# Retention group norm moved into the tile loop of a two-layer RetNet and HGRN2 decoder step

## The reference, cut to what matters

```python
mu = jnp.mean(o, axis=-1, keepdims=True)
var = jnp.mean(jnp.square(o - mu), axis=-1, keepdims=True)
on = (o - mu) * lax.rsqrt(var + GN_EPS) * gn_g.reshape(RET_HEADS, RET_DV)
o = jax.nn.silu(g) * on.reshape(bsz, l, RET_V)
return o @ w_out, s
```

## Time and profile before

| | |
|---|---|
| median of 3 runs | 1620.12 us (1617.95 to 1620.16) |
| profiled execution | 1618.11 us, span 1616.3 us |
| TensorE | busy 1570.4 us, 97% of the span |
| VectorE | 621.4 us, 38% |
| ScalarE | 422.5 us, 26% |
| mean granted TensorE clock | 0.998 of full speed |
| moved by DMA | 514.93 MB, 319 GB/s over the span |

### The profile page before, as it was taken

How to read it: one execution, slowest core, us unless ns; L and a number is a source line. 1 busy time by engine, 2 the same in 40 slices (tenths; PEclk the granted TensorE clock), 3 DMA queues, 4 the chain that set the end, 5 groups by cost and what they waited for, 6 DMA issues and landing times.

```text
span 1616.3 us, 32138 instructions
## 1 busy us (share of the span) xinstructions
PE 1570.4 (97%) x14356; PEld 931.8 (58%) x14356; DVE 621.4 (38%) x942; ACT 422.5 (26%) x608; POOL 79.7 (5%) x107
## 2 busy tenths in 40 slices
PE   7999999999999988999999999999999999999997
PEld 7888887999999988973333333333333333333332
DVE  6566576576655899542121101101111011011114
ACT  4444554444445475741000000010000000100001
POOL 1122221000000012001000000000000000000001
PEclk9999999999999999999999999999999999999999
DMA  9577879445455455269999999999999999999993
GB/s 357 211 274 294 293 269 395 169 157 182 152 179 193 157 170 178 101 269 344 428 413 405 429 402 398 426 415 409 424 394 429 421 392 425 420 396 426 390 428 131
DMA packets 138232, 514.93 MB, mean 319 GB/s; under 512 B 6700, under 2 KB 61172, under 8 KB 129780
## 3 DMA queue, kind: packets, MB, share of 16 engines
q1 hardware_dynamic: 117780, 447.93, 70.4%
q0 software_dynamic: 15824, 57.97, 9.7%
q10 hardware_dynamic: 4496, 7.02, 1.2%
HBM read 472.43 MB, written 40.47 MB: 317 GB/s over the span
## 4 chain that ended last, share of the span: by engine, by line
PE 85%; DVE 8%; ACT 1%; issue 1%; DMA 1%; POOL 0%; ACTq 0%; DVEq 0%
PE ps L1905 83%; DVE ring_low_parts L1338 1%; DVE ring L1387 1%; PE ps L2051 1%; DVE ring L1641 1%; DMA ring<-in_state_retention 1%; ACT ring_low_parts L980 1%; DVE arena L1631 1%; DVE ring L1614 0%; DVE ring L1613 0%; DVE ring L1586 0%; DVE arena L1333 0%; DVE arena L1565 0%; ACT ring L1103 0%; DVE expert_arena L1872 0%
## 5 line engine op out<-in xcount | busy, mean ns | idle before, releaser
L1905 PE MATMUL ps<-ring,expert_x_turned 128*32 128x448 f32 x5376 | 508.1, 539 | 0.0
L1905 PEld LDWEIGHTS ps<-ring,expert_x_turned 128*32 128x32 f32 x5376 | 174.5, 110 | 330.7 <-issue 330.7
L1905 PE MATMUL ps<-normed_high,ring_low_parts 128*128 128x264 f32 x1344 | 265.9, 289 | 6.7 <-DVE arena L1333 3.0
L1905 PE MATMUL ps<-ring,expert_hidden_turned 128*32 128x512 f32 x2496 | 269.3, 592 | 0.0
L980 ACT CAST ring_low_parts<-ring 128x1024 fp32r<-128x1024 f32 (+2 forms) x180 | 180.0, 1001 | 241.9 <-PE ps L1905 240.8
L1338 DVE TENSOR_TENSOR ring_low_parts<-ring,ring_low_parts 128x1024 fp32r<-128x1024 f32 (+2 forms) x180 | 207.9, 1163 | 76.4 <-ACT ring_low_parts L980 76.4
L1905 PEld LDWEIGHTS ps<-normed_high,ring_low_parts 128*128 128x128 f32 x1344 | 216.0, 190 | 8.2 <-issue 3.6
L1837 DVE TENSOR_TENSOR expert_arena<-expert_arena,ps 128x1344 f32<-128x1344 f32 x16 | 24.9, 1554 | 504.5 <-PE ps L1905 504.5
L1905 PEld LDWEIGHTS ps<-ring,expert_hidden_turned 128*32 128x32 f32 x2496 | 81.1, 110 | 185.8 <-issue 185.8
L1905 PE MATMUL ps<-normed_low,ring_low_parts 128*128 128x264 f32 x640 | 160.5, 286 | 0.0
L1905 PE MATMUL ps<-h_parts,ring_low_parts 128*128 128x264 f32 x1056 | 130.0, 285 | 0.2 <-DVE h_parts L1322 0.2
(11 more groups left out here) (290 smaller groups left out, 1185.2 us busy)
## 6 DMA issues: line engine op xcount, KB each, us to landing
ring<-in_moe_w_gate SPq DMA_DIRECT2D x64, 1792.0 KB, 13.4
ring<-in_moe_w_down SPq DMA_DIRECT2D x48, 2048.0 KB, 16.9
ring<-in_moe_w_up SPq DMA_DIRECT2D x48, 1792.0 KB, 14.2
expert_piece_slot<-in_moe_w_up SPq DMA_DIRECT2D x16, 1792.0 KB, 15.1
ring<-in_ret_w_in SPq DMA_DIRECT2D x8, 2048.0 KB, 11.0
ring<-in_state_retention POOLq DMA_DIRECT2D x32, 512.0 KB, 7.1
out_ret_s<-ring POOLq DMA_DIRECT2D x32, 512.0 KB, 4.2
ring<-in_hg_w_in SPq DMA_DIRECT2D x8, 2048.0 KB, 7.9
```

What stands on the lines that cost most here:

```text
L1905: return nc.tensor.matmul(out, lhsT, rhs, start=first, stop=last)
```

## The change

- For heads 0 to 2 the group norm moves into the loop. `NORM_TILE` says after which tile each of its four TensorE steps comes: head 0 after 18, 19, 21, 22, head 1 after 27, 29, 30, 33, head 2 after 37, 38, 39, 40.
- A sum over a head is now made in two steps: `mup` (and `vap` for the squares) multiplies the head's four tiles by 32 columns each, every tile into its own column group of one bank; ScalarE copies the bank to `std`; then `mu` (`var`) multiplies by ones over all 128 rows, which adds up the four parts and gives every row the sum. So the four spreading matmuls and `rowsel` go. In layer 1, `hsel` takes the place of `rowsel`.
- Root and reciprocal run for each head (`norm_root` on ScalarE, `normalized` on VectorE, in `group_std`). `group_std` lies where GpSimd will put its zeros, so GpSimd waits for the scaling of the last head (`scaled_ok`).
- The gate of heads 0 to 2 is one operation a tile (gate times gain times `oT`) in place of gain times gate and a multiplication over the head. High and low parts of heads 0, 1 and 2 are made in tiles 37 and 38, 41 and 42, 45 and 46.
- The last head's norm comes behind the loop, interleaved with the output projection. Its blocks are reordered: tiles 0 to 3 with k 0 to 5 and k 6 to 11 (heads 0 to 2), then (0, k 12 to 15), (1, 12 to 15), (2, 12 to 15), (4, 0 to 7), (3, 12 to 15), (4, 8 to 15), then tiles 5 to 7 in halves.
- The three `keep_busy` of the group norm go; that ahead of the dense layer stays.

```diff
+for _h, _tiles in enumerate(((18, 19, 21, 22), (27, 29, 30, 33), (37, 38, 39, 40))):
+    for _kind, _t in zip(("mup", "mu", "vap", "var"), _tiles):
+        NORM_TILE[(_kind, _h)] = _t
+NORM_BANK = {("mup", 0): 4, ("mu", 2): 4, ("var", 2): 4, ("mup", 3): 4, ("vap", 3): 4, ("mu", 3): 6, ("var", 3): 6}
...
-        for i in range(8):
-            for k in (0, 8):
-                blocks.append((("wo", i), ("rwo", i // 2), 0, 256, 16, P * (i % 2), k, k + 8, 0))
+        for i, k0, k1 in [(i, k0, k0 + 6) for i in range(4) for k0 in (0, 6)] + \
+                [(0, 12, 16), (1, 12, 16), (2, 12, 16), (4, 0, 8), (3, 12, 16), (4, 8, 16)] + \
+                [(i, k0, k0 + 8) for i in range(5, 8) for k0 in (0, 8)]:
+            blocks.append((("wo", i), ("rwo", i // 2), 0, 256, 16, P * (i % 2), k0, k1, 0))
...
             filled(pool, ("sot", RH - 1))
+            pool.wait_ge(scaled_ok, RH)
             nc.gpsimd.memset(hq_pad, 0.0).then_inc(hq_zero, 1)
...
+            def norm_part(kind, h):
+                filled(act, (kind, h))
+                frees(A.copy(std[:, :], bank((kind, h))[:, 0:NT]), (kind, h))
+            def norm_square(h):
+                freed(act, ("mu", h))
+                A.activation(o_sq, oT[:, 4 * h:4 * h + 4, :], ACT.Square).then_inc(sq_ok, 1)
+            def norm_root(h):
+                filled(act, ("var", h))
+                if h:
+                    act.wait_ge(scaled_ok, h)
+                frees(A.activation(group_std, bank(("var", h))[:, 0:NT], ACT.Sqrt, bias=eps_g), ("var", h))
...
+            norm_part("mup", last)
+            for n in range(W0, F0):
+                if n == W0 + 2:
+                    norm_part("vap", last)
+                    norm_root(last)
+                if n == W0 + 4:
+                    act.wait_ge(scaled_ok, RH)
+                    head_high(last)
+                high_part(n + FPL)
+                if n == W0:
+                    norm_square(last)
+                    A.activation(table_mark[:, 0:1], eps_n, ACT.Sqrt)
...
+                if j < 4 * RH - 4:
+                    i = V.scalar_tensor_tensor(out=oT[:, j, :], in0=oT[:, j, :], scalar=gain, in1=gT[:, j, :],
+                                               op0=ALU.mult, op1=ALU.mult)
+                else:
+                    i = V.tensor_scalar(gT[:, j, :], gT[:, j, :], gain, None, ALU.mult)
...
+            def centred(h):
+                filled(dve, ("mu", h))
+                frees(V.tensor_tensor(o_head(h), o_head(h), bank(("mu", h))[:, 0:NT].unsqueeze(1).to_broadcast([P, 4, NT]),
+                                      ALU.subtract), ("mu", h))
+            def normalized(h):
+                freed(dve, ("var", h))
+                link(V.reciprocal(group_std, group_std))
+                V.tensor_tensor(o_head(h), o_head(h), group_std.unsqueeze(1).to_broadcast([P, 4, NT]), ALU.mult)\
+                    .then_inc(scaled_ok, 1)
...
+                if kind in ("mup", "vap"):
+                    claim(name)
+                    for e in range(4):
+                        x = oT[:, 4 * h + e, :] if kind == "mup" else o_sq[:, e, :]
+                        i = mm(ps[32 * e:32 * e + 32, FILL[name][0], 0:NT], col_gn[:, 0, :], x)
+                else:
+                    freed(pe, ("mup" if kind == "mu" else "vap", h))
+                    claim(name)
+                    i = mm(bank(name)[:, 0:NT], ones, std[:, :])
+                close(i, name)
...
+            norm_product("mup", RH - 1)
+            for n in range(W0, F0):
+                ready = (lambda k: pe.wait_ge(o_ok, k // 4 + 1)) if n in (W0, W0 + 1, W0 + 8) else None
+                between = (lambda: norm_product("mu", RH - 1)) if n == W0 else \
+                    (lambda: norm_product("vap", RH - 1)) if n == W0 + 2 else None
+                product(n, o_hi, o_lo, ready, between)
+                if n == W0 + 2:
+                    norm_product("var", RH - 1)
```

More of the change, by code:

```diff
@@ L221, in retention_fills @@
             add((("sot", g), 5))
+        for name in norms_after(t, "mup", "mu", "vap", "var"):
+            add((name, NORM_BANK.get(name, 5)))
     for t in range(8 * RH + 16):
         retention_fills(t)
[L225 to L229, removed]
+    for kind in ("mup", "mu", "vap", "var"):
+        add(((kind, RH - 1), NORM_BANK[(kind, RH - 1)]))
     for i in range(8):
@@ L1049, in _ @@
                         A.activation(S, S, ACT.Copy, scale=GAMMA[hd]).then_inc(unit_decayed, 1)
[L1050 to L1072, removed]
+                for kind, hd in norms_after(t, "mup", "vap", "var"):
+                    if kind == "var":
+                        norm_root(hd)
+                    else:
+                        norm_part(kind, hd)
+                if h == RH and j in (5, 9, 13):
+                    act.wait_ge(gated_ok, j // 4)
+                    head_high(j // 4 - 1)
+            last = RH - 1
+            norm_part("mup", last)
[10 more added lines that the diff above has]
+                    A.activation(table_mark[:, 0:1], eps_n, ACT.Sqrt)
+                if block_closes(n):
+                    i = blocks[n][0][1]
+                    freed(act, ("wo", i))
+                    gain_high(1, h_hi, i)
+                    if i % 2:
+                        square(1, i // 2)
             for n in range(F0, F1):
@@ L1474, in _ @@
                           ("sot", hd))
[L1476 to L1500, removed]
@@ L1501, in _ @@
-            for i in range(9):
-                if i < 8:
+                for _, hd in norms_after(t, "mu"):
+                    centred(hd)
+            gate(4 * RH - 1)
+            last = RH - 1
+            centred(last)
+            pending = []
+            for n in range(W0, F0):
+                i = blocks[n][0][1]
+                if n == W0 + 1:
+                    dve.wait_ge(gated_ok, RH)
+                    dve.wait_ge(sq_ok, RH)
+                    link(V.tensor_tensor(o_head(last), o_head(last), gT[:, 4 * last:4 * last + 4, :], ALU.mult))
+                if n == W0 + 2:
+                    normalized(last)
+                if n == W0 + 4:
+                    head_low(last)
+                if block_closes(n):
@@ L1934, in mean_square, with product @@
                 close(i, ("ms", n))
-            def product(n, x_hi, x_lo, ready=None):
+            def product(n, x_hi, x_lo, ready=None, between=None):
                 name, _, _, _, _, _, k0, k1, base = blocks[n]
@@ L2089, in _ @@
                     sample_turn(hd)
[L2090 to L2116, removed]
+                for kind, hd in norms_after(t, "mup", "mu", "vap", "var"):
+                    norm_product(kind, hd)
+            norm_product("mup", RH - 1)
+            for n in range(W0, F0):
+                ready = (lambda k: pe.wait_ge(o_ok, k // 4 + 1)) if n in (W0, W0 + 1, W0 + 8) else None
+                between = (lambda: norm_product("mu", RH - 1)) if n == W0 else \
+                    (lambda: norm_product("vap", RH - 1)) if n == W0 + 2 else None
+                product(n, o_hi, o_lo, ready, between)
+                if n == W0 + 2:
+                    norm_product("var", RH - 1)
             for n in range(F0, F1):
```

75 lines of the change are left out of this document (55 added, 20 removed).

## The result

The changed kernel takes 1636.55 us in the median of four runs (1632.0 to 1645.71). The kernel before, run beside it, takes 1619.29. The ratio is 1.0103, with a 95% interval of 1.0078 to 1.0128. That is slower, and 14.2 us above the forecast of 1622.3; it lies outside the range of 1607 to 1627.

The account below looks back on a forecast made before the run. TensorE was taken as the bound in retention, with VectorE as full around the group norm. Terms 64.8 - 70.9 + 8.6 - 0.3 = +2.2 us took the median from 1620.12 to 1622.3; range with rival 1: 1607 to 1627.

Parts of the forecast that it names:

- the big term: Before output tile 6: the fourth weight piece, beside the zeros at 0.0925 MB/us, comes late and TensorE idles 12.1 us.
- 2.75 us of issue and landing: Fourth output piece: time added to its 22.7 us transfer, derived from a piece loaded alone in 8.2 us.
- Clock: Behind the idle time before output tile 6, a half-speed stretch costs 2.0 us, with bounds 1.7 and 3.4.
- the old slow stretch: Output projection of the kernel before: 3.4 us at half speed, costing 1.7 us, counted as removed.
- The tiles: Retention tiles: added norm matmuls and waits, less absorbed waits, cost 8.6 us by the last gate tile; bounds 5 and 14.
- fetch of a sample state: Retention loop near 215: its two waits and lost matmul overlap, 3.3 us together, taken as gone.
- A packed group: Group norm sums: four matmuls of 264 columns on four column groups, taken as 0.6 us.
- The later stages: Dense layer's first block: one cast's subtraction less before the last low part, -0.3 us.
- rival 2: Tiles 37 to 47: VectorE doesn't keep up, pair 15 waits for memory, 5 us more, 1628; chance 0.09.
- rival 3: Packing fails for these shapes: 8 groups at 1.2 us more, 1632; chance 0.02.
- The table loads: ScalarE: four added loads hidden behind TensorE work, except a quarter microsecond in tile 34.
- The norm's removal: Between retention and output projection: 21.2 us of group norm, a 1.04 us wait and slow clock go, 23.9 us.

Follow-up runs that it names:

- experiment 1: Changed kernel with the buffer of zeros moved to other memory, so GpSimd's store does not wait for the last head; 1628.7 us, ratio 1.0044.
- experiment 2: Changed kernel with GpSimd's zeros held until the last output tile is done; 1630.1 us, ratio 1.0049.
- experiment 3: Kernel before, with only GpSimd's zeros held back until output tile 0 is done; 1635.32 us, ratio 1.0078.
- experiment 5: Changed kernel with the zeros stored in five parts of 2 MB, each issued when a weight piece has landed; 1619.28 us, ratio 0.9972.
- experiment 4: Changed kernel with the zeros asked for in rows of 256 values, meant to give 1 KB packets; 1639.4 us, ratio 1.0114.
- Experiment 6: On experiment 5: head 0's mean in another bank, heads 0 and 1 scaled after the pair update, low parts later; 1610.98 us, ratio 0.9915.

## Why the prediction failed

**The mechanism of the big term was right, its size was not.** The forecast had TensorE idle before tile 6, ended by a cast that waits for the fourth piece, with zeros beside it packet for packet; experiments 1, 2, 3 and 5 show the store as the cause. The step said that the piece is there 25.4 us after its request and that TensorE then idles 12.1 us. Measured: 32.74 and 19.35, 7.2 us more. Of the piece's extra 7.3 us, the transfer made 3.3: summed by microseconds its last packet left near 311, so 2.1 MB took 26.0 us, 0.081 MB/us, where I had 0.0925 and 22.7 us. My packet of the other queue had 3.7 KB, from retention states; a packet of zeros has 4.1. The rest, 4.0 us, is in the term that I took as 2.75 us of issue and landing. It was 4.4 us until the first packet and 2.4 from the last packet to the landing: I had taken it from a load that met no full queue. With the store out of the way (experiment 5) the median fell by 24.9 us, from 1644.19 to 1619.28; the wait and its clock are 21.5 of it, and the other 3.4 are not assigned.

**Clock.** I let the clock fall once, behind the long wait, for 2.0 us; 2.2 were measured. But I also had waits of 1.8 and 1.85 us in my own sum, and the earlier trace rows show such a wait with a fall behind it. In the profiled execution the waits of 2.14 and 2.06 us brought a fall each, 1.7 us twice. This step was missing. I subtracted the old slow stretch and did not ask what its successors would bring. A fall is not certain, though: six profiles have these four waits in the tiles (the changed kernel twice, experiments 1, 2, 4 and 5), and the clock fell behind 6 of the 12 waits of 2.1 us and behind 1 of the 12 of 1.7. In experiment 1, for one, TensorE waited 2.08 us until 254.68, and the mean granted clock from 255 to 259 was 1.00. So by these counts a wait of 2.1 us brought 0.9 us of slow clock on average.

**The tiles.** Forecast +8.6 us by T0, measured +12.9. The waits were right one by one: 1.5, 1.8 and 1.85 us foretold, 1.67, 2.14 and 1.74 measured, and no fetch of a sample state is left among the long waits. A packed group cost 0.59 us from its start to the next (256.04 to 256.63), for my 0.6. The 4.3 us over are 1.7 of clock, 0.4 in the three waits, about 1.2 by which this execution was late before the first changed tile, and 1.0 not assigned. Experiment 6 took 5.4 us off experiment 5 here by order alone, so most of these waits were a matter of where an operation stands, not of its length.

**The later stages.** Forecast -0.3, in the profiled execution +11.2. Most of it is the stretch of low clock at 742 us. TensorE's starts on either side of it, in the changed kernel and then in the kernel before:

```profile
742.96 3.33 PE L1971 MATMUL ps<-cst 128*128 128x512 f32 x4 [0.48 <-DVE expert_arena L1831]
...
759.57 2.84 PE L1971 MATMUL ps<-ring,expert_x_turned 128*32 128x448 f32 x28
...
726.78 1.74 PE L1905 MATMUL ps<-cst 128*128 128x512 f32 x4 [0.48 <-DVE expert_arena L1765]
...
735.70 10.73 PE L1905 MATMUL ps<-ring,expert_x_turned 128*32 128x448 f32 x112
```

The changed kernel was 16.2 us behind at the first and 23.9 at the second: 7.7 us. The stretch at 575 cost nothing: the lag was 16.13 us ahead of it (575.58 against 559.45) and 16.12 behind it (594.56 against 578.44), and VectorE was busy 6.97 of its 7 us, as it was in the same 7 us of the kernel before. Two waits of 1.44 and 0.96 us for expert weights, near 1574 and 1584, make most of the rest. Part of such a difference belongs to single executions: two profiles of the kernel before are 2.25 us apart at the first expert (726.78 and 729.03) and 6.2 at the end. In the median the late clock is less: the four clocks have a median of 0.9885, that is 38 us at half speed. If 27 of these lie before 330 us, as in both profiles, and about 4 at the kernel's very end, where the kernel before has 3.5 too, the other 7 cost some 3 us. Why the clock fell at 742 us is open. TensorE's instructions ahead of the fall are the same as in the kernel before, where it stays at 2.4 GHz. A mere delay isn't enough: experiment 3 ended 17.7 us later than the kernel before, near the changed kernel's lag, and its profile has two stretches of 3.4 us behind 330 and none of 17. Experiment 4 is closer still: there TensorE has the changed kernel's own instructions and is 17.9 us behind the kernel before near 700, and its profile too has two of 3.4 us and none of 17.

**The sum for the profiled execution.** Forecast +2.2 us. Adding 4.3 in the tiles, 7.2 of wait, 1.7 + 0.2 of clock, 0.5 in the output blocks and 11.5 later gives 27.6, which is 1645.71 less 1618.11. For the medians, the forecast of +2.2 us stands against 1636.55 less 1619.29, or +17.3: 15.1 over. The stage's 9.6 and the tiles' 4.3 are 13.9 of it. With 3 for the late clock that is already 1.8 too much; the four runs differ by up to 13.7 us, and finer than that I can't divide the median.

**The rivals.** VectorE not keeping up (rival 2) and the packing (rival 3) decided nothing: no wait for memory stood in pair 15, and the groups cost 0.59 us. The table loads cost TensorE one wait of 0.30 us, at 192.85 in tile 34, where I had a quarter of a microsecond; no drain behind a load shows (the load at 190.93 took 1.28 us, and the root began at 192.23). The norm's removal was worth what was forecast: with the store and the order mended, the kernel is 13.2 us faster than before (1610.98 against 1624.2).

## What to carry to other kernels

When a change holds back one large transfer, find every small-packet load that it will now meet, and price it packet for packet, with the wait at the head of a full queue measured from such a case; then ask which piece TensorE needs next. A bulk store that nobody waits for for a long time can be cut into parts that each start when a piece has landed: of the four places and forms tried here for the zeros (the change, experiments 1, 2 and 5) it was the only one that left no wait for weights. And each new wait of about 2 us on TensorE should be priced with the chance of a half-speed stretch behind it: here 1.7 us in half of the cases, so that a wait of 2 us cost 2 or nearly 4.

## What the runs showed of the hardware

- A load whose queue is idle, beside a full software queue, saw its first packet 4.4 us after issue (280.63 to 285). In experiments 1 and 3 the same piece, requested at 277.74 and 277.61, had its first packets between 281 and 282 and between 282 and 283.
- The queues alternated one packet for one (807 to 809, 796 to 802) although one packet was four times as large. The loser's share was 0.083 of 0.414 MB/us.
- A store from a broadcast source, written as rows of 1 KB, still went out in packets of 4.1 KB (experiment 4: 308 packets, 1.26 MB).
- A wait of 2.1 us on TensorE was followed by 3.4 us at 1.2 GHz in 6 of 12 cases, one of 1.7 us in 1 of 12.
- TensorE's clock was at 1.2 GHz for 17 us (742 to 759) in a stretch where it was busy 97% of the time, in both profiles of the changed kernel and in neither of the kernel before, with the same instructions there. The cause stays open.
